# One load per expert for gate and up, and a new column order in the first block of the output product

## What is computed

```
y = (sigmoid(ga) * pool + sigmoid(gb) * (o @ w_attn_out)) @ w_out          # x = x + y
comb = weight of each of 32 experts for each token, nonzero for 2 of them
act  = silu(h @ w_g[e]) * (h @ w_u[e])                                      # 1024 -> 128, per expert
x    = x + sum over e of (act * comb[e]) @ w_d[e]                           # 128 -> 1024
```

## Time and profile before

| | |
|---|---|
| median of 3 runs | 1279.79 us |
| the profiled execution | 1279.34 us, with a span of 1277.5 us |
| TensorE busy | 1227.9 us (96%) |
| attention ends, output product begins | 793 us |
| experts | about 1036 to 1232 us |
| rows back, norm, output | 1238 us to the end |

### The profile page before, as it was taken

How to read it: one execution, slowest core, us unless ns; L and a number is a source line. 1 busy time by engine, 2 the same in 40 slices (tenths; PEclk the granted TensorE clock), 3 DMA queues, 4 the chain that set the end, 5 groups by cost and what they waited for, 6 DMA issues and landing times.

```text
span 1277.5 us, 21420 instructions
## 1 busy us (share of the span) xinstructions
PE 1227.9 (96%) x7577; PEld 1068.0 (84%) x7577; DVE 917.7 (72%) x2179; ACT 511.9 (40%) x1117; POOL 440.8 (35%) x740
## 2 busy tenths in 40 slices
PE   6999999999999999998999999999999979999987
PEld 6999999999999999998777766999788858887753
DVE  5667888889998999874677776232666668877747
ACT  6554323232321112224666554000432247766634
POOL 5803565676873115654000010210011233433310
PEclk9999999999999999998999999999999989999998
DMA  7201322222223221103000231944321469999749
GB/s 274 72 28 56 99 65 79 42 79 42 71 56 121 90 70 53 34 1 104 2 1 17 63 95 58 324 136 162 116 83 47 153 227 334 364 336 348 291 172 366
DMA packets 79457, 163.84 MB, mean 128 GB/s; under 512 B 12418, under 2 KB 48082, under 8 KB 78210
## 3 DMA queue, kind: packets, MB, share of 16 engines
q1 hardware_dynamic: 64977, 128.84, 29.6%
q0 software_dynamic: 12656, 27.62, 6.5%
q10 hardware_dynamic: 1728, 6.10, 1.2%
HBM read 137.86 MB, written 39.21 MB: 139 GB/s over the span
## 4 chain that ended last, share of the span: by engine, by line
PE 84%; DMA 6%; POOL 3%; ACT 3%; DVE 2%; SPq 1%; issue 1%; POOLq 0%; ACTq 0%; DVEq 0%
PE bank L921 12%; PE bank L920 12%; PE bank L922 12%; PE bank L1133 5%; PE bank L1115 3%; PE bank L1214 3%; PE bank L1208 3%; PE bank L1346 2%; PE bank L1051 2%; PE bank L1225 2%; PE bank L1226 2%; PE bank L1227 2%; DMA region_t<-ffn_input_scratch,small_i 2%; DMA region_h<-in_wd 2%; PE bank L1210 2%; PE bank L1361 1%
## 5 line engine op out<-in xcount | busy, mean ns | idle before, releaser
L1961 DVE MAX8 small<-region_kv 128x8 f32<-128x272 f32 (+4 forms) x241 | 190.2, 828 | 47.6 <-DVE region_kv L1966 47.5
L920 PE MATMUL bank<-h_hi,w_hi 128*128 128x384 f32 (+1 forms) x576 | 196.1, 340 | 0.0
L921 PE MATMUL bank<-h_lo,w_hi 128*128 128x384 f32 (+1 forms) x576 | 196.1, 340 | 0.0
L1966 DVE MATCH_REPLACE8 region_kv<-small,region_kv 128x272 f32<-128x272 f32 (+4 forms) x241 | 195.5, 818 | 0.0
L922 PE MATMUL bank<-h_hi,w_lo 128*128 128x384 f32 (+1 forms) x576 | 194.4, 338 | 0.0
L920 PE MATMUL bank<-w_hi,h_hi 128*128 128x256 f32 x448 | 128.8, 288 | 1.0 <-ACT region_q L1511 1.0
L2323 POOL TENSOR_TENSOR w_lo<-w_stage,w_hi 128x512 fp32r<-128x512 f32 x64 | 80.8, 1295 | 141.2 <-ACT w_hi L1450 141.1
L922 PE MATMUL bank<-w_hi,h_lo 128*128 128x256 f32 x448 | 125.9, 281 | 0.0
L921 PE MATMUL bank<-w_lo,h_hi 128*128 128x256 f32 x448 | 125.9, 281 | 0.0
L922 PEld LDWEIGHTS bank<-h_hi,w_lo 128*128 128x128 f32 x576 | 108.7, 189 | 0.0
L921 PEld LDWEIGHTS bank<-h_lo,w_hi 128*128 128x128 f32 x576 | 108.2, 188 | 0.6
(11 more groups left out here) (350 smaller groups left out, 3066.5 us busy)
## 6 DMA issues: line engine op xcount, KB each, us to landing
w_stage<-in_w_in SPq DMA_DIRECT2D x72, 256.0 KB, 3.2
region_kv<-in_xa SPq DMA_DIRECT2D x16, 512.0 KB, 5.8
region_h<-in_wg SPq DMA_DIRECT2D x15, 512.0 KB, 5.2
region_h<-in_wu SPq DMA_DIRECT2D x15, 512.0 KB, 13.6
region_h<-in_wd SPq DMA_DIRECT2D x15, 512.0 KB, 19.3
region_q<-in_wd SPq DMA_DIRECT2D x12, 512.0 KB, 19.0
region_q<-in_wg SPq DMA_DIRECT2D x12, 512.0 KB, 6.0
region_q<-in_wu SPq DMA_DIRECT2D x12, 512.0 KB, 14.2
```

What stands on the lines that cost most here:

```text
L920: mm(out, st_hi(k), mv_hi(k), start=(k == 0), stop=False)
L921: mm(out, st_hi(k), mv_lo(k), start=False, stop=False)
L1961: nc.vector.max(m8[:, q, :], x).then_inc(dve_c, 1)
L1966: nc.vector.match_replace(x, m8[:, q, :], x, TAKEN).then_inc(dve_c, 1)
```

## The change

Two edits. The gate and up weights of an expert are laid side by side in DRAM when the inputs are prepared, one row of 8 KB per partition, and one transfer of 1 MB takes the place of two of 512 KB. The slot counts two loads per use, 32 in place of 48. And in block 0 of the output product the three units are computed in the order 1, 2, 0; the first two wait for all groups but the last, the third for all.

```
+        OUT3 = [[1, 2, 0]] + [[0, 1, 2]] * (KD - 1)
...
             def load_gate_up(e):
                 s = e % NSLOT
-                sp.dma_start(eslot[s][:, 0:1024], a["wg"][e]).then_inc(ew_in[s], 16)
-                sp.dma_start(eslot[s][:, 1024:2048], a["wu"][e]).then_inc(ew_in[s], 16)
+                sp.dma_start(eslot[s][:, 0:2048], a["wgu"][e]).then_inc(ew_in[s], 16)
...
-            pe.wait_ge(a_oe, NG_ALL)
+            pe.wait_ge(a_oe, NG_ALL - 1)
             for c in range(KD):
                 pe.wait_ge(wao_low, c + 1)
-                for j, (c0, c1) in enumerate(TOK3):
-                    u = 3 * c + j
+                for n, j in enumerate(OUT3[c]):
+                    c0, c1 = TOK3[j]
+                    u = 3 * c + n
+                    if u == 2:
+                        pe.wait_ge(a_oe, NG_ALL)
                     if u >= 4:
                         pe.wait_ge(b6_evac, u - 3)
...
             def expert_upper(e):
-                act.wait_ge(ew_in[e % NSLOT], 48 * (e // NSLOT + 1))
+                act.wait_ge(ew_in[e % NSLOT], 32 * (e // NSLOT + 1))
...
             for c in range(KD):
                 dve.wait_ge(sbi_in[c % 2], 16 * (c // 2 + 1))
                 dve.wait_ge(mu_in[c % 2], 16 * (c // 2 + 1))
-                for j, (c0, c1) in enumerate(TOK3):
-                    u = 3 * c + j
+                for n, j in enumerate(OUT3[c]):
+                    c0, c1 = TOK3[j]
+                    u = 3 * c + n
                     dve.wait_ge(b6_done, u + 1)
```

More of the change, by code:

```diff
@@ L1402, in _ @@
                     pe.wait_ge(te_evac, 2 * NE + 1 + it)
-                    pe.wait_ge(ov_w, 48 * it + 48)
+                    pe.wait_ge(ov_w, 32 * it + 32)
                     gate_up(0, 0, 0)
@@ L2555, in _ @@
                     row = pool.snap((code // NE) * (P * NE - NE) + code + P * NE, min_val=0, max_val=NE * (TOK - P) + NE - 1)
-                    for o, src in ((0, a["wg"]), (1024, a["wu"])):
-                        pool.dma_start(eslot[0][:, o:o + 1024], src[bass.ds(ex, 1), :, :].rearrange("o p c -> p (o c)")).then_inc(ov_w, 16)
+                    pool.dma_start(eslot[0][:, 0:2048], a["wgu"][bass.ds(ex, 1), :, :].rearrange("o p c -> p (o c)")).then_inc(ov_w, 16)
                     pool.dma_start(e_down(0), a["wd"][bass.ds(ex, 1), :, :].rearrange("o p f -> p (o f)")).then_inc(ov_w, 16)
@@ L2628 @@
         "rbias": np.broadcast_to(np.concatenate([f["b_router_group"][0], f["b_router_expert"][0]]), (P, NG + NE)),
-        "wg": f["w_expert_gate"][0].reshape(NE, KD, P, DE).transpose(0, 2, 1, 3).reshape(NE, P, D),
-        "wu": f["w_expert_up"][0].reshape(NE, KD, P, DE).transpose(0, 2, 1, 3).reshape(NE, P, D),
+        "wgu": np.concatenate([f["w_expert_gate"][0].reshape(NE, KD, P, DE).transpose(0, 2, 1, 3).reshape(NE, P, D),
+                               f["w_expert_up"][0].reshape(NE, KD, P, DE).transpose(0, 2, 1, 3).reshape(NE, P, D)], axis=2),
         "wd": f["w_expert_down"][0],
```

## The result

The changed kernel takes 1295.48 us (median of 4 runs, 1291.39 to 1297.88), against 1280.53 (1278.62 to 1281.43) for the kernel before on the same chip: ratio 1.011, 95% interval 1.0092 to 1.0128. It is 15 us slower. The forecast was 1276.0.

A forecast was written before the change was run, and what follows sets the result against it. TensorE was taken to bound most of the kernel, with full DMA engines delaying down weights among the experts. 1279.34 - 1.5 (order) - 2.9 (wide load) + 0.8 (gathers) = 1275.7, taken as 1276.0 us; range 1272.8 to 1279.8.

The forecast's parts named there:

- What bounds the kernel now: TensorE over most of the kernel; among the experts, full DMA engines make casts wait 29.3 us for down weights.
- New order in block 0: Output product: TensorE runs on after attention without its 1.51 us idle time; gain 1.5 us, at worst 1.2.
- The fifth unit: Output product, near 809 us: needs the bank of the first evacuation, which waits for the gate's transfer; 5 us of cover.
- What the gathers pay: Experts: gathers land later behind SyncE's wider packets, 0 to 1.6 us; 0.8 taken, charged once.
- rival B: Experts: gathers 2.45 us late set the pace, (15.8 + lateness) / 3 per expert; slower, 1283.4 us; chance 0.10.
- the slack of 0.9 us: Experts, steady part: a gather lands by the median at 1146.9 for transposes at 1147.79, taken to absorb lateness.
- One load in place of two: Experts 9 to 28: 8 KB packets save 0.145 us each on full engines; gain 2.9 us (2.0 to 4.0).
- Rival A: Experts: wider rows bring nothing beside row traffic, only the 1.5 us stays; 1278.3 us; chance 0.20, shared with another rival.

The follow-up runs named there:

- 7: Changed kernel with two loads of 4 KB rows again and an expert's tokens spread evenly over the partitions: 1268.43 us, 0.9905 of the kernel before.
- 1: Kernel before with only the new column order; gate and up stay two loads of 4 KB rows: 1278.33 us, ratio 0.9983.
- 12: Kernel before with the new order, 4 KB rows, and up weights from expert 7 on issued by ScalarE on a third queue: 1302.52 us, ratio 1.0155.
- 11: Changed kernel with gate, up and down as one load of 12 KB rows from expert 7 on: 1294.42 us, 1.0096 of the kernel before.
- 4: Changed kernel with each scatter issued one turn later, so the gather goes out earlier: 1287.39 us, 1.0055 of the kernel before.
- 9: Changed kernel, 8 KB rows, with tokens spread over the partitions and gathers issued ahead of the scatter: 1269.49 us, 0.9895 of the kernel before.
- 10: Changed kernel with two loads of 4 KB rows again, tokens spread and gathers issued ahead of the scatter: 1270.00 us, 0.9903 of the kernel before.
- 3: Changed kernel with its single 1 MB load moving 256 rows of 4 KB: 1279.24 us, 0.9989 of the kernel before.
- 2: Kernel before with only the single gate and up load of 8 KB rows, old column order: 1299.06 us, ratio 1.0146.

## Why the prediction was wrong

**What bounds the kernel now**: right: 7 shows that engines with more to carry than the others were the bound, and evening them out took all 29.3 us of cast waits away, down to TensorE's 5.57.

**New order in block 0**: right. 1.5 us forecast, 1.83 earlier in the profile, 2.2 (0.9 to 3.6) in 1. The fifth unit didn't stall. The other 1.1 us by which expert 5 is earlier in the profile after I don't credit to it: the transposes of expert 0 lie between 1040.4 and 1044.4 us in kernels with the same start.

**What the gathers pay** is the step that failed. I took +0.8 with an upper end of 1.6, and charged it once. It is +4.2, beyond even rival B's 2.45, and it is paid in every turn of a loop of three experts. Rival B's mechanism came true, at a chance of 0.10, though its 1283.4 us was far too low; with 4.2 in its formula the pace is 6.67 (measured 6.75), with the gathers of 12 it is (7.0 + 13.8) / 3 = 6.93 (measured 7.00), with those of 11 (7.0 + 12.9) / 3 = 6.63 (6.65). Two errors made x small, as I read it. I priced the foreign packets at the mean over all of SyncE's, with their number held at 23, as if a gather met a fixed crowd. But with a turn after each packet, GpSimd's queue moves its rows at a rate: if the other side's turn gets longer, each of its own 16 or so rows per expert waits longer, and what the last scatter left over is still ahead of the next gather. In 4 such a backlog builds up between expert 10 and 20; the rate itself was not measured. Without the loop the width costs 2.3 us (9 against 10), also more than my upper end. And I weighed the slack of 0.9 us against a single delay, where each gather of the loop has to fit into it. That it was nearly used up stands in the trace of before: TensorE already waits for gathers there (1136 to 1217 us):
```profile
PE bank L1333 <- DMA region_t<-ffn_input_scratch,small_i: 2.9, 4, 1.7
```
The Trainium skill (DMA: Bandwidth & Descriptors, Queues, rings and completion order) says that an engine drains a whole packet of one queue before it switches; 3 and 12 agree, the first for the width of the rows, the second for the number of queues. What it calls a packet is typically 9 to 17 descriptors; that the packets of the profile, one per row here, are these turns no run shows. I had cited it and then took the middle between it and its opposite.

**One load in place of two** failed as well: none of the 2.9 us came. What it did to the casts can't be seen in the time, since they no longer bind. The 4% of 8 KB packets were read where nothing but loads ran. Beside row traffic it turned round here: SyncE's queue, 1060 to 1140 us, before and after (packets, MB, share of 16 engines):
```profile
q1 hardware_dynamic: 5542, 20.08, 68.6%
```
```profile
q1 hardware_dynamic: 3533, 19.03, 70.1%
```
That is 20.08 MB in 0.686 x 16 x 80 = 878 us of packet time, 22.9 GB/s, and then 19.03 in 897, 21.2: 7% less where I forecast more. 3 has 22.5 (20.15 MB at 70.1%). With tokens spread, 7 has 23.8 and 9 has 23.5. Rival A (no gain there) was nearer than the forecast. But it isn't the 8 KB packet by itself that is slow. The same view of 12, where all packets are of 4 KB (SyncE's queue, ScalarE's), and of 11, where they are of 12 KB:
```profile
q1 hardware_dynamic: 3464, 12.49, 47.1%
q10 hardware_dynamic: 1737, 6.32, 22.0%
```
```profile
q1 hardware_dynamic: 1767, 19.00, 63.2%
```
Both queues of 12 together have 21.3 GB/s, as little as after, and 11 has 23.5.

The cast waits that vanished are part of the same. Down loads, 1060 to 1140 us, of before and of 2:
```profile
region_q<-in_wd SPq DMA_DIRECT2D x6, 512.0 KB, 19.1
```
```profile
region_q<-in_wd SPq DMA_DIRECT2D x6, 512.0 KB, 10.2
```
SyncE's queue, seven slots deep, is served sooner with the larger packets, though also asked for less at the slower pace, and GpSimd's queue, three buffers deep, later. As I read it, the same shortage of engine time now shows where the slack is least.

Not settled: what sets the bytes per packet time beside row traffic (21.2 to 23.8 GB/s), and why 12 KB rows delay a gather no more than 8 KB rows. A longer turn explains 3 and 12 in sign, not the 13 us of both 8 and 12 KB. One reading that no run tests: the weights of an expert come to an engine as 24 packets before, as 16 after (8 of 8 KB, 8 of 4 KB) and as 8 in 11, beside some 16 rows of GpSimd's on a low engine. If one foreign packet passes per row, 16 of 24 get ahead before, but all of them after and in 11, and with two queues in 12 as well; and more than all there can't be.

## What to carry to other kernels

The row width of a bulk load is not only a matter of its own rate: on shared engines it can set how long a small transfer of another queue waits (4 against 8 KB did here, 8 against 12 KB did not), and if a loop hangs on that transfer, a few microseconds come back in every turn. So before a bulk queue's packets are made larger, or a queue is added, measure the slack of the shallowest buffer beside it, and charge a delay once per turn of that loop. And where the DMA share falls well short of one while a load is still late, look for uneven engines first: here one constant that spreads the rows was worth some 10 us (7 against 1), and after it the wide load cost nothing more once the gather also had slack.

## What the runs showed of the hardware that was not expected

- Alone, 8 KB packets ran 4% faster than those of 4 KB (427 and 411 GB/s); beside gathers and scatters SyncE's queue moved 7% fewer bytes per packet time with them (21.2 and 22.9 GB/s). Packets of 12 KB had 23.5 there, and those of 4 KB on two queues 21.3.
- Rows of 8 KB in the place of 4 KB made a gather on another queue land 2.3 us later (10.0 and 7.7 us, 9 and 10), though TensorE never waited for it.
- A third queue with 4 KB packets made gathers 13.7 us late, the most of all kernels, and the total rate fell to 305 to 320 GB/s.
- Packets of 12 KB cost a gather no more than those of 8 KB (12.9 and 13.0 us from issue to transposes), at mean DMA shares of 0.88 to 0.90.
- In the profile after, TensorE's granted clock fell once among the experts, to the lower level of 1.2 GHz, behind a wait of 2.31 us for the gather of expert 17: the down product after it took 3.31 us in the chain, that of expert 26 took 1.72. That is some 1.6 us, once. Waits of about 2 us in 2, 4 and 11 (1.8, 2.3, 1.9 at the longest) left it at 1.00 there; 12 has 0.94. After:
```profile
1149.00:1154.00 5.00, 5.00 (x20) 2.83 (x19) 2.19 (x4) 3.65 (x6) 0.00 (x0) 0.66 0.81 293
```
